# Differential attention of a two-layer hybrid block: new weight sum, new unit order, seven key tiles on GpSimd

## Chip, cores and metric

The kernel runs on one core of one Trainium2 chip. The metric is the device time of the program in microseconds. PE is the TensorE matmul queue and PEld its weight load, DVE is VectorE, ACT is ScalarE, POOL is GpSimd, and SP is the queue that issues most DMAs.

## The reference

Two layers of a block with three attention branches (gated linear, differential, sliding window), an output projection and a SwiGLU. Only the differential branch is touched:

```
s = einsum('bhctd,bhcmd->bhctm', q, k) * DIFF_DH ** -0.5      # 4 heads, c = 2 maps of width 32
p = softmax(s, axis=-1)
w = p[:, :, 0] - lam * p[:, :, 1]
o = einsum('bhtm,bhmv->bhtv', w, v)                            # v is 64 wide
out = rms_norm(o, g) * (1 - lam_init)                          # per head, eps 1e-6
```

There are 256 context and 1024 latent tokens, so 10 tiles of 128. In layer 0 context rows attend to context keys, latent rows to all 1280 keys; in layer 1 only latent rows are needed. Everything is float32.

## The kernel before

The program runs stage after stage with a barrier between them; `differential_attention` runs once per layer, after the gated linear attention and ahead of the sliding window. Each engine has its own instruction stream and works it in program order; engines meet only at semaphores (`wait_ge`, `then_inc`).

The unit of work is one head of one query tile (`u`). A pair of tiles (`i`) has 8 units. Layer 0 has 8 short context units (256 keys) and 32 latent units (1280 keys); layer 1 has 32 latent units. `staggered` writes the steps `r` of a software pipeline: in step `r` an engine does the first part of unit `r` and later parts of earlier units, and `live(lag)` says whether unit `r - lag` exists. The context units and the latent units are two pipelines, each filled and drained by itself.

One unit, before:

- PE L1723: scores of map 0, then of map 1, into the two PSUM halves `SC[:, c]` (3 matmuls each). A half is free again once its exponential is done.
- DVE L1852, L1854: row maximum and its negative. ACT L1777: exponential with the row sum into `den`.
- DVE L1859, L1861: reciprocals of both sums, and minus lambda times the second. POOL L1828: `W = E0 / den0`. DVE L1867: `W += E1 * r1`, over all keys.
- PE L1710: transposes of W in three groups of 3, 4 and 3 tiles. Groups 0 and 2 use PSUM bank `TR[:, 0]`, group 1 uses `TR[:, 1]`. ACT L1785 copies each group to `WT` (`take`).
- PE L1747: ten products of a value tile (128x64) with WT, accumulated in `TR[:, 1]`. DVE L1872 copies the 64x128 result into `oT`.

In step `r` PE issues score 0 and score 1 of `r`, groups 0, 1 and 2 of `r-2`, and the products of `r-3`. ACT does `take` 0 and 1 of `r-2`, exponential 0 of `r`, `take` 2 of `r-2`, exponential 1 of `r`. The stage starts once all constants, the values and the keys have landed; the values are transposed first (L1702, L1765). After the last unit the RMS norm is made on full 128x1280 tiles: squares (L1802), a product with the block mean (L1758), square root (L1805), reciprocal (L1878), product (L1880), for two head pairs.

Of the kernel before, what the change touches and what calls it, by code (L numbers as in the profile page):

```python
# [1595 lines left out]
def differential_attention(nc, t, res, layer, tiles):  # L1596

    with nc.cleanup_on_exit(), ExitStack() as ctx:
# [5 lines left out]
        LAG = 3  # L1610
# [3 lines left out]
        first_latent = CTX_TILES // 2  # L1614
        KEYCH = [(0, 512), (512, 512), (1024, 256)]
# [13 lines left out]
        eps = sb(nm + "eps", [P, 1])  # L1629
        mx = sb(nm + "mx", [P, 2])  # L1630
        ng = sb(nm + "negmax", [P, 2])
        den = sb(nm + "den", [P, 2, 2])
        rden = sb(nm + "rden", [P, 2, 2])
        r1 = sb(nm + "r1", [P, 2])
        E = sb(nm + "e", [P, 2, 2, T])
        W = sb(nm + "w", [P, 2, T])
# [4 lines left out]
        const_in, k_in, eps_set = sem("const_in"), sem("k_in"), sem("eps_set")  # L1641
        q_in = [sem(f"q_in{s}") for s in range(2)]
        lam, lam_exp = sem("lam"), sem("lam_exp")
        v_turned, v_copied = sem("v_turned"), sem("v_copied")
        scores, max_done, neg_done, exp_done, rden_done, r1_done, w0_done, w_done = (
            sem("scores"), sem("max_done"), sem("neg_done"), sem("exp_done"), sem("rden_done"), sem("r1_done"), sem("w0_done"), sem("w_done"))
        turned = [sem(f"turned{g}") for g in range(3)]
        copied = [sem(f"copied{g}") for g in range(3)]
        pv_done, o_done, passed = sem("pv_done"), sem("o_done"), sem("passed")
        sq_done, mean_done, rms_done, inv_done, normed, stored = (  # L1650
            sem("sq_done"), sem("mean_done"), sem("rms_done"), sem("inv_done"), sem("normed"), sem("stored"))
# [4 lines left out]
        def done(i, u):  # L1656

            return (i - first_pair) * UN + u + 1
# [4 lines left out]
        def groups(i):  # L1663

            return [(0, 1), (1, 1)] if is_ctx(i) else [(0, 3), (3, 4), (7, 3)]

        def third(i, u):

            return done(i, u) - (first_latent - first_pair) * UN

        def stagger(eng, step):
            if first_pair < first_latent:
                staggered(eng, first_pair, first_latent, UN, LAG, step)
            staggered(eng, first_latent, end_pair, UN, LAG, step)

        @block.sync
        def _(sp):
            heads = t["heads"]
            for j, part in enumerate((0, 1, 0)):
                sp.dma_start(ks[32 * j:32 * j + 32, :, :].bitcast(F32), heads[part, HEAD_DK:HEAD_DK + 2 * P, 0:T].rearrange("(a p) n -> p a n", p=32)).then_inc(k_in, 16)  # L1680

            def body(i, first):
                for s in range(2):
                    if not first:
                        sp.wait_ge(scores, 2 * (done(i, s * H + H - 1) - UN))
                    for j, part in enumerate((0, 0, 1)):
                        sp.dma_start(qs[32 * j:32 * j + 32, s, :, :].bitcast(F32),
                                     heads[part, HEAD_DQ:HEAD_DQ + 2 * P, bass.ds(i * 2 * P + s * P, P)].rearrange("(a p) n -> p a n", p=32)).then_inc(q_in[s], 16)
# [7 lines left out]
        def _(pe):  # L1696
            pe.wait_ge(const_in, 80)
            for g, (i, a, n) in enumerate(VG):
                if g >= 2:
                    pe.wait_ge(v_copied, g - 1)  # L1700
                for c in range(n):
                    mm = pe.transpose(TR[:, g % 2, c * P:(c + 1) * P], vT[:, i, (a + c) * P:(a + c + 1) * P], ident[:, :])  # L1702
                mm.then_inc(v_turned, 1)
            pe.wait_ge(v_copied, len(VG))
            pe.wait_ge(k_in, 48)

            def turn(i, u, g):
                a, n = groups(i)[g]
                for c in range(n):
                    mm = pe.transpose(TR[:, g % 2, c * P:(c + 1) * P], W[:, u % 2, (a + c) * P:(a + c + 1) * P], ident[:, :])  # L1710
                mm.then_inc(turned[g], 1)

            def step(i, r, live):
                if live(0):
                    s, h = r // H, r % H
                    if h == 0:
                        pe.wait_ge(q_in[s], (i - first_pair) * 48 + 48)
                    for c in range(2):

                        wait_count(pe, exp_done, 2 * (done(i, r) - 1) + c - 1)  # L1720
                        for a, n in KEYCH[:1 if is_ctx(i) else 3]:
                            n = min(n, N_CTX) if is_ctx(i) else n
                            mm = pe.matmul(SC[:, c, a:a + n], qs[:, s, 2 * h + c, :], ks[:, 2 * h + c, a:a + n], start=True, stop=True)  # L1723
                        mm.then_inc(scores, 1)
                if live(2):
                    u = r - 2
# [8 lines left out]
                    if not is_ctx(i):  # L1735
                        pe.wait_ge(copied[0], done(i, u))
                        turn(i, u, 2)
                if live(3):
                    u, h = r - 3, (r - 3) % H

                    pe.wait_ge(copied[1], done(i, u) + (1 if live(2) else 0))
                    wait_count(pe, o_done, done(i, u) - 1)
                    if not is_ctx(i):
                        pe.wait_ge(copied[2], third(i, u))
                    tiles_ = groups(i)[-1][0] + groups(i)[-1][1]
                    for c in range(tiles_):
                        mm = pe.matmul(TR[64 * (h % 2):64 * (h % 2) + 64, 1, 0:P], V[:, c, 64 * h:64 * h + 64],  # L1747
                                       WT[:, u % 2, c * P:(c + 1) * P], start=(c == 0), stop=(c == tiles_ - 1))
                    mm.then_inc(pv_done, 1)
            stagger(pe, step)  # L1750


            for i in range(2):
                pe.wait_ge(sq_done, i + 1)
                for a, n in KEYCH:
                    n = min(n, tn - a)
                    if n > 0:
                        mm = pe.matmul(SC[:, i, a:a + n], block_mean[:, :], E[:, 0, i, a:a + n], start=True, stop=True)  # L1758
                mm.then_inc(mean_done, 1)

        @block.scalar
        def _(act):
            for g, (i, a, n) in enumerate(VG):
                act.wait_ge(v_turned, g + 1)
                act.copy(V[:, a:a + n, i * P:(i + 1) * P], TR[:, g % 2, 0:n * P].rearrange("p (c f) -> p c f", f=P)).then_inc(v_copied, 1)  # L1765
            act.wait_ge(lam, 4)
            act.activation(lexp[:, :], lsum[:, :], ACT.Exp).then_inc(lam_exp, 1)
            act.wait_ge(eps_set, 1)

            def step(i, r, live):  # L1770
                keys = (CTX_TILES if is_ctx(i) else TILES) * P

                def exponentials(c):
                    act.wait_ge(neg_done, 2 * (done(i, r) - 1) + c + 1)
                    if c == 0:
                        wait_count(act, w_done, done(i, r) - 2)
                    act.activation(E[:, r % 2, c, 0:keys], SC[:, c, 0:keys], ACT.Exp, bias=ng[:, c:c + 1], scale=scale,  # L1777
                                   accum_out=den[:, r % 2, c:c + 1]).then_inc(exp_done, 1)
# [8 lines left out]
                if live(2):  # L1787
# [401 lines left out]
```

## Time and profile before

| | us |
|---|---|
| median of 3 runs (4523.80 to 4535.81) | 4533.56 |
| the profiled execution, its own time | 4548.76 |
| its span, first to last instruction | 4547.0 |
| PE busy in the span | 3797.9 |
| DVE busy | 1820.1 |
| ACT busy | 1305.8 |
| POOL busy | 1246.8 |

The profile is one execution. Busy times are sums over all stages; what a stage is worth is read from its own stretch. The two differential stages lie at about 783 to 1054 us and 3149 to 3387 us. The granted TensorE clock is 1.00 for 2.4 GHz and 0.50 for 1.2 GHz.

### The profile page before, as it was taken

The numbers are of one execution on the slowest core, as the hardware profiler recorded it, in microseconds if no ns is written. First come the engines' busy times: TensorE is split into PE (matmuls) and PEld (weight loads), VectorE is DVE, ScalarE is ACT, GpSimd is POOL, SyncE is SP. The second block draws the span as 40 slices with busy tenths as digits, with TensorE's granted clock in tenths as the row PEclk, the third lists the DMA queues.
The fourth block names the chain that finished last, engine by engine and source line by source line (L and its number), as shares of the span: only waits on it lengthen the run. The fifth ranks groups of instructions, "written<-read, shape, count | busy, mean of one in ns | idle before, by whom it ended". The sixth has DMA issues, their size and how long they took to land. (4 is left out here: it accounts for less than half of the span.)

```text
span 4547.0 us, 54135 instructions
## 1 busy us (share of the span) xinstructions
PE 3797.9 (84%) x20674; PEld 3078.6 (68%) x20674; DVE 1820.1 (40%) x2680; ACT 1305.8 (29%) x2275; POOL 1246.8 (27%) x877
## 2 busy tenths in 40 slices
PE   7899597795776999999976798696968669999992
PEld 1588487573655888888861687585747548888881
DVE  1104453696754121121228005543968552122215
ACT  2211332574633101111004211332747441111111
POOL 1211321121334323223223211321213243333332
PEclk9999676797988999999998899676989889999996
DMA  7423211203142111111115223202022321111112
GB/s 255 159 83 114 82 24 35 50 11 87 37 137 86 40 33 42 42 37 37 37 58 206 93 80 122 71 13 67 18 58 45 114 83 47 51 46 50 47 37 88
DMA packets 150767, 320.53 MB, mean 70 GB/s; under 512 B 11745, under 2 KB 72033, under 8 KB 150625
## 3 DMA queue, kind: packets, MB, share of 16 engines
q1 hardware_dynamic: 127944, 260.47, 18.4%
q10 hardware_dynamic: 18456, 44.07, 2.6%
q0 software_dynamic: 4224, 14.09, 1.1%
q8 instruction: 90, 1.47, 0.1%
q14 instruction: 53, 0.43, 0.0%
HBM read 250.20 MB, written 68.39 MB: 70 GB/s over the span
## 5 line engine op out<-in xcount | busy, mean ns | idle before, releaser
L1980 POOL TENSOR_TENSOR ffn_wlo<-ffn_raw,ffn_whi 128x1024 fp32r<-128x1024 f32 x132 | 314.6, 2390 | 800.6 <-ACT ffn_whi L1951 800.6
L2044 DVE TENSOR_TENSOR ffn_hid<-ffn_up,ffn_silu 128x512 f32<-128x512 f32 (+1 forms) x110 | 70.2, 638 | 1049.4 <-PE ffn_up L127 1023.2
L1951 ACT CAST ffn_whi<-ffn_raw 128x1024 fp32r<-128x1024 f32 x132 | 136.4, 1049 | 944.7 <-PE ffn_acc L127 467.4
L2049 DVE TENSOR_TENSOR y<-ffn_acc,y 128x512 f32<-128x512 f32 x396 | 274.0, 692 | 266.6 <-PE ffn_acc L127 266.6
L125 PE MATMUL ffn_gate<-second_uhi,ffn_whi 128*128 128x512 f32 (+1 forms) x880 | 326.2, 371 | 37.3 <-POOL ffn_wlo L1980 37.3
L126 PE MATMUL ffn_gate<-second_ulo,ffn_whi 128*128 128x512 f32 (+1 forms) x880 | 325.9, 370 | 0.0
L127 PE MATMUL ffn_gate<-second_uhi,ffn_wlo 128*128 128x512 f32 (+1 forms) x880 | 325.6, 370 | 0.0
L126 PE MATMUL ffn_up<-second_ulo,ffn_whi 128*128 128x512 f32 (+1 forms) x880 | 324.2, 368 | 0.0
L125 PE MATMUL ffn_up<-second_uhi,ffn_whi 128*128 128x512 f32 (+1 forms) x880 | 324.1, 368 | 0.0
L127 PE MATMUL ffn_up<-second_uhi,ffn_wlo 128*128 128x512 f32 (+1 forms) x880 | 324.0, 368 | 0.0
L125 PE MATMUL ffn_acc<-ffn_whi,ffn_hhi 128*128 128x512 f32 x792 | 308.5, 390 | 0.0
L126 PE MATMUL ffn_acc<-ffn_wlo,ffn_hhi 128*128 128x512 f32 x792 | 308.5, 389 | 0.0
L127 PE MATMUL ffn_acc<-ffn_whi,ffn_hlo 128*128 128x512 f32 x792 | 308.4, 389 | 0.0
L611 POOL TENSOR_TENSOR in_wlo<-in_raw,in_whi 128x1024 fp32r<-128x1024 f32 x42 | 100.3, 2390 | 475.5 <-ACT in_whi L635 475.5
L125 PEld LDWEIGHTS ffn_gate<-second_uhi,ffn_whi 128*128 128x128 f32 x880 | 167.1, 190 | 66.4 <-POOL ffn_wlo L1980 38.1
L1011 PE MATMUL gla_unit<-gla_X 64*128 64x64 f32 x1120 | 209.1, 365 | 0.0
L1010 PE MATMUL gla_unit<-gla_X 64*128 64x64 f32 x1120 | 209.1, 365 | 0.0
L1010 PEld LDWEIGHTS gla_unit<-gla_X 64*128 64x128 f32 x1120 | 200.7, 277 | 7.7 <-DVE gla_A L1265 2.7
L1852 DVE TENSOR_REDUCE diff_mx<-diff_scores 128x1 f32<-128x1280 f32 (+1 forms) x144 | 196.8, 1367 | 11.5 <-PE diff_scores L1723 10.3
L1011 PEld LDWEIGHTS gla_unit<-gla_X 64*128 64x128 f32 x1120 | 200.7, 277 | 0.0
L685 DVE LOAD_MASK_SELECT in_swap<-in_stage x18 | 0.3, 14 | 497.9 <-ACT in_stage L640 497.9
L125 PE MATMUL in_acc<-second_uhi,in_whi 128*128 128x512 f32 (+1 forms) x504 | 179.9, 357 | 20.9 <-POOL in_wlo L611 20.9
(269 smaller groups left out, 9172.0 us busy)
## 6 DMA issues: line engine op xcount, KB each, us to landing
ffn_raw<-w_ffn_dram SPq DMA_DIRECT2D x132, 512.0 KB, 3.5
in_raw<-w_in_dram SPq DMA_DIRECT2D x42, 512.0 KB, 3.5
norm_input_ada_w<-w_ada_dram SPq DMA_DIRECT2D x10, 2048.0 KB, 8.1
norm_ffn_ada_w<-w_ada_dram SPq DMA_DIRECT2D x8, 2048.0 KB, 8.8
proj_scratch<-in_stage ACTq DMA_DIRECT2D x24, 640.0 KB, 2.9
ada_w<-w_ada_dram SPq DMA_DIRECT2D x6, 2048.0 KB
heads_scratch<-in_shi ACTq DMA_DIRECT2D x18, 640.0 KB, 3.0
heads_scratch<-in_slo ACTq DMA_DIRECT2D x18, 640.0 KB, 4.2
```

The lines of the kernel that those rows point to most:

```text
L125: pe.matmul(out, st_hi, mv_hi, start=start, stop=False)
L126: pe.matmul(out, st_hi, mv_lo, start=False, stop=False)
L127: return pe.matmul(out, st_lo, mv_hi, start=False, stop=stop)
L611: pool.tensor_tensor(wlo[:, s, :, :], raw[:, s, :].rearrange("p (k n) -> p k n", k=KT), whi[:, s, :, :].bitcast(F32), ALU.subtract).then_i ...
L685: dve.stream_shuffle(swap[:, s, :], x, MASK).then_inc(swapped, 1)
L1010: pe.matmul(fslot(s, c), x[UP, :], halves(x, m)[UP, :, 1, :], start=True, stop=True)
L1011: mm = pe.matmul(bslot(s, c), x[DOWN, :], halves(x, m)[DOWN, :, 0, :], start=True, stop=True)
L1852: dve.reduce_max(mx[:, c:c + 1], SC[:, c, 0:keys], AX.X).then_inc(max_done, 1)
L1951: act.copy(whi[:, j % 3, :], raw[:, j % 3, :]).then_inc(w_hi, 1)
L1980: pool.tensor_tensor(wlo[:, j % 3, :], raw[:, j % 3, :], whi[:, j % 3, :].bitcast(F32), ALU.subtract).then_inc(w_ready, 1)
L2044: dve.tensor_tensor(hf[:, c, 0:tn], UP[:, c, 0:tn], sg[:, c, 0:tn], ALU.mult).then_inc(mul_done, 1)
L2049: dve.tensor_tensor(Y[:, tt, cols], ACC[:, half, :], Y[:, tt, cols], ALU.add).then_inc(y_added, 1)
```

## The change

It rewrites the body of `differential_attention`. The weights are no longer divided by the first sum: `W = E0 + ratio * E1` with `ratio = -lam * den0 / den1`, and the first sum enters only the norm, where its square multiplies epsilon. The parts:

- Weights: POOL multiplies and then adds over the first 7 key tiles (896 columns, two instructions); DVE does the last 3 tiles (384 columns) in one instruction. W has 4 buffers in place of 2.
- Order: on PE score 0 of `r`, group 2 of `r-3`, products of `r-4`, score 1 of `r`, groups 0 and 1 of `r-2`. On ACT exponential 0 of `r`, `take` 0 and 1 of `r-3`, exponential 1 of `r`, `take` 2 of `r-3`. The drain is 4 steps in place of 3.
- Products: the ten key tiles go in two chains of five, one to PSUM partitions 0 to 63 and one to 64 to 127, issued in turn; DVE copies one half and adds the other.
- Start: queries of the first tile are loaded first, keys by head with a semaphore each, values by a DMA of the ACT queue; the values are transposed and lambda is made after the first unit's scores.
- Norm: means and square roots on 128x20 numbers, spread to full tiles by small products.

The core of the diff (removed lines are shown where the order on ACT changes; elsewhere the listing above has them):

```
-        LAG = 3
+        TURN, REST, WEIGH = 2, 3, 4
...
+        OWN = 7
...
+        W = sb(nm + "w", [P, 4, T])
...
+                    if first and s == 0:
+                        for h in range(H):
+                            keys(h)
...
+            def values():
+                pe.wait_ge(v_in, 16)
+                for g, (i, a, n) in enumerate(VG):
+                    if g >= 2:
+                        pe.wait_ge(v_copied, g - 1)
+                    for c in range(n):
+                        mm = pe.transpose(TR[:, g % 2, c * P:(c + 1) * P], vT[:, i, (a + c) * P:(a + c + 1) * P], ident[:, :])
+                    mm.then_inc(v_turned, 1)
...
                 if live(0):
+                    if r % H == 0:
+                        pe.wait_ge(q_in[r // H], (i - first_pair) * 48 + 48)
+                    if isinstance(i, int):
+                        pe.wait_ge(k_in[r % H], 48)
+                    score(i, r, 0)
+                if live(REST) and not is_ctx(i):
+                    u = r - REST
+                    pe.wait_ge(copied[0], done(i, u))
+                    pe.wait_ge(w2_done, third(i, u))
+                    turn(i, u, 2)
+                if live(WEIGH):
+                    u, h = r - WEIGH, (r - WEIGH) % H
+                    pe.wait_ge(copied[1], done(i, u) + (1 if live(REST) else 0))
+                    pe.wait_ge(copied[0], done(i, u))
+                    wait_count(pe, o_done, done(i, u) - 1)
+                    if not is_ctx(i):
+                        pe.wait_ge(copied[2], third(i, u))
+                    n = (groups(i)[-1][0] + groups(i)[-1][1]) // 2
+                    for c in range(n):
+                        for half in range(2):
+                            k = half * n + c
+                            mm = pe.matmul(TR[64 * half:64 * half + 64, 1, 0:P], V[:, k, 64 * h:64 * h + 64],
+                                           WT[:, u % 2, k * P:(k + 1) * P], start=(c == 0), stop=(c == n - 1))
+                    mm.then_inc(pv_done, 1)
+                if live(0):
+                    score(i, r, 1)
+                    if first_step(i, r):
+                        values()
+                if live(TURN):
+                    u = r - TURN
                     pe.wait_ge(w_done, done(i, u))
                     wait_count(pe, copied[0], done(i, u) - 1)
                     if not is_ctx(i):
                         wait_count(pe, copied[2], third(i, u) - 1)
                     turn(i, u, 0)
+                    wait_count(pe, copied[1], done(i, u) - 1)
                     wait_count(pe, o_done, done(i, u) - (1 if live.starts and u == 0 else 2))
                     turn(i, u, 1)
             stagger(pe, step)
...
+                for c in tiles:
+                    mm = pe.matmul(TR[:, i, 2 * c:2 * c + 2], E[:, 0, i, c * P:(c + 1) * P], block_mean[:, 0:P:64], start=True, stop=True)
                 mm.then_inc(mean_done, 1)
+            for i in range(2):
+                pe.wait_ge(inv_done, i + 1)
+                for c in tiles:
+                    for half in range(2):
+                        mm = pe.matmul(SC[64 * half:64 * half + 64, i, c * P:(c + 1) * P], rs[:, i, c, half:half + 1].to_broadcast([P, 64]), ident[:, :], start=True, stop=True)
+                mm.then_inc(spread_done, 1)
...
+            act.dma_start(vT[:, :, :], t["proj"][T_DV * P:(T_DV + 2) * P, 0:T].rearrange("(i p) n -> p i n", p=P)).then_inc(v_in, 16)
...
-                if live(2):
-                    take(r - 2, 0)
-                    take(r - 2, 1)
                 if live(0):
                     exponentials(0)
-                if live(2) and not is_ctx(i):
-                    take(r - 2, 2)
+                if live(REST):
+                    take(r - REST, 0)
+                    take(r - REST, 1)
                 if live(0):
                     exponentials(1)
+                if live(REST) and not is_ctx(i):
+                    take(r - REST, 2)
+                if first_step(i, r):
+                    act.wait_ge(lam, 4)
+                    act.activation(lexp[:, :], lsum[:, :], ACT.Exp).then_inc(lam_exp, 1)
+                    for g, (j, a, n) in enumerate(VG):
+                        act.wait_ge(v_turned, g + 1)
+                        act.copy(V[:, a:a + n, j * P:(j + 1) * P], TR[:, g % 2, 0:n * P].rearrange("p (c f) -> p c f", f=P)).then_inc(v_copied, 1)
             stagger(act, step)
...
+                    n = min(keys, OWN * P)
+                    w = W[:, u % 4, 0:n]
+                    pool.tensor_scalar(w, E[:, u % 2, 1, 0:n], ratio[:, u % 2:u % 2 + 1], 1.0, ALU.mult, ALU.mult).then_inc(w1_done, 1)
+                    pool.wait_ge(w1_done, done(i, u))
+                    pool.tensor_tensor(w, w, E[:, u % 2, 0, 0:n], ALU.add).then_inc(w_done, 1)
             stagger(pool, step)
...
+                if live(0):
+                    maximum(i, r, 0)
                 if live(1):
                     u, b = r - 1, (r - 1) % 2
+                    at = (tile_of(i, u), slice(u % H, u % H + 1))
+                    dve.wait_ge(exp_done, 2 * done(i, u))
+                    dve.reciprocal(rden[:, b:b + 1], den[:, 1, at[0], at[1]].rearrange("p a b -> p (a b)")).then_inc(rden_done, 1)
+                    dve.wait_ge(rden_done, done(i, u))
+                    wait_count(dve, w_done, done(i, u) - 2)
+                    dve.scalar_tensor_tensor(ratio[:, b:b + 1], den[:, 0, at[0], at[1]].rearrange("p a b -> p (a b)"), nlam[:, 0:1], rden[:, b:b + 1], ALU.mult, ALU.mult).then_inc(ratio_done, 1)
+                    if not is_ctx(i):
+                        wait_count(dve, turned[2], third(i, u) - 4)
+                        dve.wait_ge(ratio_done, done(i, u))
+                        dve.scalar_tensor_tensor(W[:, u % 4, OWN * P:T], E[:, u % 2, 1, OWN * P:T], ratio[:, b:b + 1],
+                                                 E[:, u % 2, 0, OWN * P:T], ALU.mult, ALU.add).then_inc(w2_done, 1)
+                if live(0):
+                    maximum(i, r, 1)
+                    if first_step(i, r):
+                        difference()
+                if live(WEIGH):
+                    u = r - WEIGH
+                    h = u % H
+                    rows, other = slice(64 * (h % 2), 64 * (h % 2) + 64), slice(64 - 64 * (h % 2), 128 - 64 * (h % 2))
+                    at = bass.ds(i * 2 * P + u // H * P, P)
                     dve.wait_ge(pv_done, done(i, u))
+                    dve.tensor_copy(oT[rows, h // 2, at], TR[rows, 1, 0:P]).then_inc(half_done, 1)
+                    dve.wait_ge(half_done, done(i, u))
+                    dve.tensor_tensor(oT[rows, h // 2, at], oT[rows, h // 2, at], TR[other, 1, 0:P], ALU.add).then_inc(o_done, 1)
             stagger(dve, step)
...
+            seen = slice(tiles[0], TILES)
+            dve.tensor_tensor(dsq[:, seen, :], den[:, 0, seen, :], den[:, 0, seen, :], ALU.mult).then_inc(dsq_done, 1)
+            dve.wait_ge(dsq_done, 1)
+            for i in range(2):
+                dve.wait_ge(mean_done, i + 1)
+                dve.scalar_tensor_tensor(ms[:, i, seen, :], dsq[:, seen, 2 * i:2 * i + 2], EPS,
+                                         TR[:, i, 2 * tiles[0]:2 * TILES].rearrange("p (c a) -> p c a", a=2), ALU.mult, ALU.add).then_inc(ms_done, 1)
+            for i in range(2):
+                dve.wait_ge(rms_done, i + 1)
+                dve.reciprocal(rs[:, i, seen, :], ms[:, i, seen, :]).then_inc(inv_done, 1)
             for i in range(2):
                 o = oT[:, i, t0:t0 + tn]
```

## Rows read from the trace of the kernel before

**Rows 1.** The page: the granted TensorE clock over the span's 40 slices.

```profile
PEclk9999676797988999999998899676989889999996
```

**Rows 2.** Busy time by stretch: start us:end us, length, PE, PEld, DVE, ACT, POOL, clock, DMA.

```profile
842.00:862.00 20.00, 14.92 (x48) 11.09 (x49) 16.02 (x23) 12.61 (x21) 4.00 (x3) 0.50 0.07 20
862.00:1014.00 152.00, 147.12 (x1022) 120.32 (x1021) 145.66 (x226) 114.41 (x198) 37.28 (x28) 1.00 0.05 14
1090.00:1240.00 150.00, 124.91 (x770) 102.08 (x769) 125.81 (x292) 113.78 (x259) 53.70 (x72) 1.00 0.18 41
```

**Rows 3.** Groups of DVE instructions, 862 to 1014 us: busy, mean ns, idle before.

```profile
L1852 DVE TENSOR_REDUCE diff_mx<-diff_scores 128x1 f32<-128x1280 f32 x56 | 83.1, 1485 | 1.0 <-PE diff_scores L1723 0.5
L1867 DVE SCALAR_TENSOR_TENSOR diff_w<-diff_e,diff_r,diff_w 128x1280 f32<-128x1280 f32 x28 | 43.5, 1552 | 0.4 <-issue 0.3
L1854 DVE TENSOR_SCALAR diff_negmax<-diff_mx 128x1 f32<-128x1 f32 x56 | 8.6, 154 | 1.9
L1872 DVE COPY diff_oT<-diff_tr 64x128 f32 (+1 forms) x29 | 8.3, 285 | 2.7 <-PE diff_tr L1747 2.3
L1861 DVE TENSOR_SCALAR diff_r<-diff_rden,diff_nlam 128x1 f32<-128x1 f32 x28 | 6.0, 214 | 1.0
```

**Rows 4.** Instructions in order of time, one full-clock unit: start us, us, engine.

```profile
907.35 0.80 PEld L1710 LDWEIGHTS diff_tr<-ident,diff_w 128*128 128x128 f32 x7
...
908.00 1.02 ACT L1785 COPY diff_wT<-diff_tr 128x384 f32<-128x384 f32 x2 [1.26 <-PE diff_tr L1710]
...
909.07 2.40 PE L1747 MATMUL diff_tr<-diff_wT,diff_V 128*64 128x128 f32 x20
```

**Rows 5.** The same view, latent units of layer 0 at the half clock.

```profile
840.00 1.49 DVE L1852 TENSOR_REDUCE diff_mx<-diff_scores 128x1 f32<-128x1280 f32 x1 [1.07 <-PE diff_scores L1723]
...
843.18 1.44 PE L1723 MATMUL diff_scores<-diff_k,diff_q 96*128 96x512 f32 x3 [2.15 <-ACT diff_e L1777]
...
844.65 1.49 DVE L1852 TENSOR_REDUCE diff_mx<-diff_scores 128x1 f32<-128x1280 f32 x1 [1.39 <-PE diff_scores L1723]
...
846.37 1.33 ACT L1777 ACTIVATE diff_e<-diff_scores,diff_negmax 128x1280 f32<-128x1280 f32 x1 [1.65 <-DVE diff_negmax L1854]
...
853.19 1.33 ACT L1777 ACTIVATE diff_e<-diff_scores,diff_negmax 128x1280 f32<-128x1280 f32 x1
...
854.51 0.48 ACT L1785 COPY diff_wT<-diff_tr 128x384 f32<-128x384 f32 x1
...
859.96 2.39 PE L1747 MATMUL diff_tr<-diff_wT,diff_V 128*64 128x128 f32 x10
```

**Rows 6.** The same view, small products of the linear attention in two column halves.

```profile
705.14 4.12 PE L1057 MATMUL gla_unit<-ident,gla_rs 128*64 128x128 f32 x40
```

**Rows 7.** Groups of POOL instructions over the whole span.

```profile
L535 POOL TENSOR_TENSOR norm_attention_h<-norm_attention_h,norm_attention_lng 128x1024 f32<-128x1024 f32 x18 | 43.0, 2387 | 114.5 <-ACT norm_attention_h L491 114.5
L1828 POOL TENSOR_SCALAR diff_w<-diff_e,diff_rden 128x1280 f32<-128x1280 f32 x64 | 85.2, 1332 | 298.0 <-DVE diff_rden L1859 290.2 <-PE diff_tr L1710 4.2 <-issue 3.6
```

**Rows 8.** The last latent unit's first maximum and the end of the loop, layer 0.

```profile
1008.65 1.49 DVE L1852 TENSOR_REDUCE diff_mx<-diff_scores 128x1 f32<-128x1280 f32 x1
...
1024.77 0.29 DVE L1872 COPY diff_oT<-diff_tr 64x128 f32<-64x128 f32 x1 [2.51 <-PE diff_tr L1747]
```

**Rows 9.** Start of the stage: layer 0, DMA of 785 to 812 us; then layer 1.

```profile
805.61 0.30 DVE L1836 TENSOR_TENSOR diff_lprod<-diff_lamv 128x32 f32<-128x32 f32 x2 [26.13 <-DMA diff_block_mean<-block_mean_dram]
DMA packets 2831, 6.07 MB, mean 225 GB/s; under 512 B 256, under 2 KB 1792, under 8 KB 2831
3149.65 0.44 SPq L1680 DMA_DIRECT2D diff_k<-heads_scratch  x1
3176.41 2.50 PE L1723 MATMUL diff_scores<-diff_k,diff_q 96*128 96x512 f32 x6 [0.46 <-ACT diff_V L1765]
```

**Rows 10.** The norm at the end of the stage, layer 0, in order of time.

```profile
1030.23 8.15 DVE L1878 RECIPROCAL diff_e<-diff_e 128x1280 f32<-128x1280 f32 x1 [5.17 <-ACT diff_e L1805]
```

**Rows 11.** One line: small DVE instructions with two SBUF inputs; ns min/median/max.

```profile
L426 DVE SCALAR_TENSOR_TENSOR norm_attention_nmu<-norm_attention_mv,norm_attention_rstd x36: 159/160/2380, 1292.6 to 3713.1; 128x1 f32<-128x1 f32 x36
```

More of the change, by code:

```diff
@@ L1678, in _, with queries, keys @@
             heads = t["heads"]
-            for j, part in enumerate((0, 1, 0)):
-                sp.dma_start(ks[32 * j:32 * j + 32, :, :].bitcast(F32), heads[part, HEAD_DK:HEAD_DK + 2 * P, 0:T].rearrange("(a p) n -> p a n", p=32)).then_inc(k_in, 16)
+            def queries(i, s):
+                for j, part in enumerate((0, 0, 1)):
+                    sp.dma_start(qs[32 * j:32 * j + 32, s, :, :].bitcast(F32),
+                                 heads[part, HEAD_DQ:HEAD_DQ + 2 * P, bass.ds(i * 2 * P + s * P, P)].rearrange("(a p) n -> p a n", p=32)).then_inc(q_in[s], 16)
+            def keys(h):
+                rows = slice(HEAD_DK + 64 * h, HEAD_DK + 64 * h + 64)
+                for j, part in enumerate((0, 1, 0)):
+                    sp.dma_start(ks[32 * j:32 * j + 32, 2 * h:2 * h + 2, :].bitcast(F32), heads[part, rows, 0:T].rearrange("(a p) n -> p a n", p=32)).then_inc(k_in[h], 16)
             def body(i, first):
@@ L1713, in step, with score @@
+            def score(i, r, c):
+                h = r % H
+                wait_count(pe, exp_done, 2 * (done(i, r) - 1) + c - 1)
+                for a, n in KEYCH[:1 if is_ctx(i) else 3]:
+                    n = min(n, N_CTX) if is_ctx(i) else n
+                    mm = pe.matmul(SC[:, c, a:a + n], qs[:, r // H, 2 * h + c, :], ks[:, 2 * h + c, a:a + n], start=True, stop=True)
+                mm.then_inc(scores, 1)
             def step(i, r, live):
                 if live(0):
-                    s, h = r // H, r % H
@@ L1716, in step @@
[L1716 to L1724, printed above, removed]
@@ L1731, in step @@
                     turn(i, u, 0)
+                    wait_count(pe, copied[1], done(i, u) - 1)
                     wait_count(pe, o_done, done(i, u) - (1 if live.starts and u == 0 else 2))
                     turn(i, u, 1)
[L1735 to L1749, printed above, removed]
@@ new lines, in maximum @@
+            def maximum(i, r, c):
+                keys = (CTX_TILES if is_ctx(i) else TILES) * P
+                n = 2 * (done(i, r) - 1) + c + 1
+                dve.wait_ge(scores, n)
+                dve.reduce_max(mx[:, c:c + 1], SC[:, c, 0:keys], AX.X).then_inc(max_done, 1)
+                dve.wait_ge(max_done, n)
+                dve.tensor_scalar(ng[:, c:c + 1], mx[:, c:c + 1], -scale, None, ALU.mult).then_inc(neg_done, 1)
+            def step(i, r, live):
+                if live(0):
+                    maximum(i, r, 0)
@@ new lines, in step @@
+                    if not is_ctx(i):
+                        wait_count(dve, turned[2], third(i, u) - 4)
[6 more added lines that the diff above has]
+                        difference()
```

135 lines of the change are left out of this document (48 added, 87 removed).

## Prediction, made blind

> **What bounds the kernel now.** I read the clock line of the page first [rows 1]: it moves between its two levels, so each stretch needs its own. Then busy time by stretch. From 862 to 1014 us the latent loop of layer 0 has the full clock with DVE busy for 145.66 of 152 us and PE for 147.12 [rows 2]. Two engines are nearly full. The groups of DVE say how full: per unit two maxima (2 x 1.485), two negatives (2 x 0.154), two reciprocals, the lambda product (0.214), the weight sum (1.552) and the copy to `oT` (0.285) [rows 3]. The 28 units in 152 us make 5.43 us each. First maximum of the first to first maximum of the last latent unit, 840.00 [rows 5] to 1008.65 [rows 8], is 168.65 us for 31 steps, 5.44 each. DVE waits for nobody longer than half a microsecond there, because each unit's chain of waits is spread over three steps: ACT does `take` 0 and 1 of an old unit before exponential 0 of the new one, so no engine waits for work of its own step.
>
> **The new order closes a ring.** I wrote down for each engine what its new stream needs, in step `r`:
>
> 1. PE: score 0 of `r`. Then group 2 of `r-3` waits for `copied[0]`, which is `take` 0 of `r-3`.
> 2. ACT issues that `take` behind exponential 0 of `r`, so it waits for maximum 0 of `r`, so for score 0 of `r`.
> 3. PE: the products of `r-4` wait for `copied[1]` of `r-3`; score 1 of `r` stands behind them.
> 4. ACT issues `take` 2 of `r-3` behind exponential 1 of `r`: that needs maximum 1, so score 1.
> 5. PE: group 0 of `r-2` waits for `copied[2]` of `r-3`, and score 0 of `r+1` stands behind groups 0 and 1.
>
> So score 0, maximum 0, exponential 0, two copies, products, score 1, maximum 1, exponential 1, one copy, seven transposes, score 0 of the next unit: all in series, with no slack from any lag. More buffers for W don't open it, since no wait in it is for W.
>
> **Its length at the half clock.**
> - Maximum start to exponential start: 844.65 to 846.37, 1.72 us [rows 5], twice.
> - Exponential to the end that releases the copy behind it: 853.19 to 854.51, 1.32 [rows 5], twice.
> - Two copies, to the first product: 908.00 to 909.07, 1.07 [rows 4]; group 2's three transposes run beside the second copy and push the products by about 0.18.
> - Products: the nearest row is 20 pairs of column halves in 4.12 us [rows 6], 0.206 a pair, if the halves of a pair overlap as there. Five pairs plus drain of the pipeline would be 1.3, ten passes without overlap 2.39 [rows 5]. The listing issues ten products of 128 columns; I take 2.3, nearer to the unpaired end.
> - One copy of 384 columns: 0.48, with handover 0.53 [rows 5].
> - Seven transposes at the 0.21 to 0.24 a pass that ten passes show [rows 5]: 1.5, plus 0.1 to start.
> - Score start to maximum start: 843.18 to 844.65, 1.47 [rows 5], twice.
>
> First half 1.72 + 1.32 + 1.25 + 2.3 + 1.47 = 8.06; second 1.72 + 1.32 + 0.53 + 1.6 + 1.47 = 6.64. Together **14.7 us a unit**. The path through `o_done` is shorter: it asks for maximum 1 and some 2 us of DVE, where exponential 1 and `take` 2 need 3.6 from the same start.
>
> **Its length at the full clock.** ACT and DVE keep their durations. Products 1.25 (twenty passes in 2.40 [rows 4]), score to maximum about 0.85 (half of the three passes' 1.44 [rows 5], and 0.13 to hand over), seven transposes 0.80 [rows 4]: **11.5 us**.
>
> **Which clock.** PE would be busy about 7.4 of 14.7 us at the half clock, and 4.2 of 11.5 at the full one. The stretch 842 to 862 had PE busy for 14.92 of 20 and stayed at 0.50; 124.91 of 150 kept 1.00 in another stage [rows 2]. Both are far above 50%, so I take the half clock.
>
> The Trainium skill ("TensorE: Matmul & The Clock Gate", section "A second HAM failure mode: psum-queue depth-cycling") says that PE's short idles between groups of matmuls make the clock go up and down instead of settling. By that rule part of the loop would have the full clock; the stretch at 0.50 here shows no such change.
>
> **The sum, against the profiled execution (4548.76 us).**
> - Latent loop, per layer: the first three steps have no work of older units, 16 us at about the 5.4 of now; the fourth is a ring without products, 12.4; 27 steps of 14.7 make 397. Then 30 us from the last unit's first maximum to the last `oT` (13.2 left of its step, four drain steps of some 4.2), where before it took 16.41 (1008.65 to 1025.06 [rows 8]). 455 against 185: +270, for two layers **+540**.
> - Context units, layer 0: the ring has no `take` 2, so only its first half closes. With a fifth of the maximum, exponential and products that leaves 3.7 us, plus 1.4 for score 1, two transposes and the next score: 5.1, against some 2.6. Eight of them +20. The start gives back part: DVE waited 26.13 us for the last constant [rows 9]; the loads are 6.07 MB at 225 GB/s [rows 9], so the first head and tile are there after about half of that, but the last keys set the fourth unit. I take -17; bounds 0 and -26. Together **+3**.
> - Start of layer 1: first scores 26.8 us after the issue of the keys (3149.65 to 3176.41 [rows 9]); now first keys and queries alone after about 13. Less 3 for the values in the first step: **-11** (bounds 0 and -14).
> - Norm: each layer loses an 8.15 us reciprocal [rows 10] and, by the durations of exponentials and scores, about 5 of full-width square root and wide mean products; it gains 20 passes for the means and 20 pairs for the spreading, about 4.3 each at 0.21 [rows 6]. The last products stay. **-8** for both (bounds -14 and 0).
> - POOL at 7 tiles: the multiply is 1332 ns for 1280 columns, the addition 2387 for 1024 [rows 7], so for 896 columns 1.01 and 2.11 (the second by the wider type of operation, nearest row). DVE's 384 columns 0.62. These 3.1 us run beside the ring: W is needed two steps later. Nothing; were the ring open, POOL would still need less than DVE.
> - DVE's new copy and addition of halves: 0.57 in place of 0.285, beside the ring: nothing.
>
> 540 + 3 - 11 - 8 = +524. The profiled execution is 15 us, 0.3%, above the median, so the sum is set on the median: 4533.56 + 524 = **5058 us**.
>
> **Rivals.**
> - *The ring at the full clock, or part of it.* Speaks for it: the loop enters from stages with their own clock, and idle time within a unit is spread in short pieces. Against: the busy share above. At 11.5 us a unit the latent loops cost +354 and starts and norm -22: 4866; with half of the loop at each clock some 4960. Chance 0.22 for anything from 4866 to 5000.
> - *Faster: no ring, DVE bounds.* This needs `take` of `r-3` to be done before exponential 0 of `r`, which decides at that one wait: if PE's group 2 of `r-3` need not stand ahead of score 1 in time, or my reading of the counts is off by a unit. Then DVE needs 2 x 1.485 + 2 x 0.154 + 0.155 + 0.21 + 0.62 + 0.57 [rows 3], 4.8 us, and PE with pairs about 4. 63 steps of -0.55 are -34, starts and norm -24: 4475. Chance 0.09.
> - *Same: that, but DVE's part of W waits for POOL.* DVE's instructions with two SBUF inputs last 160 ns as a rule and up to 2380 [rows 11], as long as the addition of POOL in the same stretch. If DVE's 384 columns waited for a multiply of 1.01 each unit it would need 5.85, and 63 x 0.4 would eat the gains: 4543 or so. Both wait for the same ratio, and DVE follows its own release sooner. Chance 0.02. The Trainium skill ("SBUF — State Buffer") has the port pair of DVE and GpSimd as an exclusive lock, held for the full instruction; in the ring this costs nothing, since DVE has over 8 us of slack a unit.
> - *Longer.* Products at 2.39 and more, each handover 0.1 longer: 16 us a unit, 5140. Chance 0.04.
>
> **How the numbers follow.** The ring at the half clock has 0.63. Its own range is 5000 to 5110: 14.7 give or take 0.9 a unit over 58 steps is 52 us. The range reaches down to 4870, which takes in the ring at the full clock, and ends at 5110. Left out are the faster case, the same, and the longer one. A measurement of this kernel can tell about 0.3% from no change. Faster 0.09, same 0.02, slower 0.89.
>
> **What would show it.** In the changed profile first maxima should stand 14.7 us apart in the latent loops (11.5 if the clock is full). PE should wait for ACT's copies to `diff_wT` ahead of the products and of group 0, and for nothing of W; ACT should wait for DVE's negatives and start its copies at once behind each exponential; DVE busy under 40% of the loop; the clock 0.50 there; POOL two instructions near 1.0 and 2.1; no reciprocal of 8 us; first scores some 13 us after the issue of loads. I am wrong if the copies lie ahead of their step's exponentials in time, or if first maxima come under 6 us apart.

## The result and the profile after

| | before, us | after, us |
|---|---|---|
| median (4 runs each) | 4534.69 | 5055.74 |
| lowest to highest | 4523.80 to 4542.01 | 5040.69 to 5060.31 |
| profiled execution: span | 4547.0 | 5052.8 |

The ratio is 1.1145 (95% interval 1.1113 to 1.1178): 11% slower. The prediction of 5058 us is 2 us off. The page of the changed kernel, busy times and clock:

```profile
PE 3908.7 (77%) x20870; PEld 3148.9 (62%) x20870; DVE 1768.8 (35%) x2750; ACT 1301.6 (26%) x2275; POOL 1385.2 (27%) x945
...
PEclk9998675555798899999998997865556988999996
```

DVE has less work than before (1820.1) and ACT as much. PE is busy for 111 us more and POOL for 138 us more, while the span is 506 us longer: most of the added time is work that waits, not more work. The low digits in the clock line, against [rows 1], are the two stages. The loop of layer 0 by stretch (columns as in [rows 2]):

```profile
880.00:1260.00 380.00, 186.95 (x935) 141.84 (x936) 123.72 (x230) 104.41 (x182) 90.07 (x52) 0.57 0.02 5
```

PE is busy for 49% and DVE for 33%, where [rows 2] had 97% and 96%. The groups of PE, ACT and DVE in the latent units of layer 0, with what ended their idle time:

```profile
L1710 PE MATMUL diff_tr<-ident,diff_w 128*128 128x128 f32 x320 | 81.5, 419 | 218.7 <-ACT diff_wT L1809 214.2 <-DVE diff_w L1896 3.8 <-DVE diff_oT L1910 0.7
...
L1801 ACT ACTIVATE diff_e<-diff_scores,diff_negmax 128x1280 f32<-128x1280 f32 x64 | 84.9, 1327 | 313.6 <-DVE diff_negmax L1880 313.6
...
L1878 DVE TENSOR_REDUCE diff_mx<-diff_scores 128x1 f32<-128x1280 f32 x63 | 93.9, 1491 | 272.7 <-PE diff_scores L1728 272.7
```

Each engine has one partner: PE waits for ACT's copies, ACT for DVE's negatives, DVE for PE's scores. That is a ring, and the order in time shows one turn of it:

```profile
1104.91 1.49 DVE L1878 TENSOR_REDUCE diff_mx<-diff_scores 128x1 f32<-128x1280 f32 x1 [4.25 <-PE diff_scores L1728]
...
1106.81 1.33 ACT L1801 ACTIVATE diff_e<-diff_scores,diff_negmax 128x1280 f32<-128x1280 f32 x1 [4.87 <-DVE diff_negmax L1880]
...
1107.19 0.62 DVE L1896 SCALAR_TENSOR_TENSOR diff_w<-diff_e,diff_ratio 128x384 f32<-128x384 f32 x1
1107.29 1.39 POOL L1854 TENSOR_SCALAR diff_w<-diff_e,diff_ratio 128x896 f32<-128x896 f32 x1 [11.44 <-DVE diff_ratio L1892]
...
1108.12 0.95 ACT L1809 COPY diff_wT<-diff_tr 128x384 f32<-128x384 f32 x2
...
1109.55 2.40 PE L1755 MATMUL diff_tr<-diff_wT,diff_V 128*64 128x128 f32 x20
...
1111.88 0.86 PE L1728 MATMUL diff_scores<-diff_k,diff_q 96*128 96x512 f32 x3
1112.77 1.49 DVE L1878 TENSOR_REDUCE diff_mx<-diff_scores 128x1 f32<-128x1280 f32 x1 [4.97 <-PE diff_scores L1728]
...
1114.58 1.33 ACT L1801 ACTIVATE diff_e<-diff_scores,diff_negmax 128x1280 f32<-128x1280 f32 x1 [5.50 <-DVE diff_negmax L1880]
...
1115.89 0.47 ACT L1809 COPY diff_wT<-diff_tr 128x384 f32<-128x384 f32 x1
...
1116.51 1.73 PE L1710 MATMUL diff_tr<-ident,diff_w 128*128 128x128 f32 x7 [3.77 <-ACT diff_wT L1809]
...
1117.89 1.42 PE L1728 MATMUL diff_scores<-diff_k,diff_q 96*128 96x512 f32 x3
1119.34 1.49 DVE L1878 TENSOR_REDUCE diff_mx<-diff_scores 128x1 f32<-128x1280 f32 x1 [4.32 <-PE diff_scores L1728]
```

Within the ring nothing overlaps; only work outside it runs beside it (W, group 2's transposes, the output). From 1104.91 to 1119.34 are 14.43 us; over the last 27 steps the first maxima stand 14.73 us apart in layer 0 and 14.64 in layer 1. DVE's wait of 4.97 ends with three score passes of 0.86 in all, so at the full clock. The clock was granted at 1.00 for short stretches, of which most fell on an idle PE: cut into pieces of half a microsecond, 880 to 1260 us has the full clock in 100 of 760, and in those PE was busy for 11% of the time, against 55% in the pieces at the half clock. By the rows of the two kernels, each stage splits like this (us; before, after, and what was forecast for the difference):

| | before | after | difference | forecast |
|---|---|---|---|---|
| layer 0: first load issued to first latent maximum | 56.5 | 58.9 | +2.4 | +3 |
| layer 1: the same | 29.5 | 16.4 | -13.1 | -11 |
| first to last latent unit's first maximum, layers 0, 1 | 168.6, 168.3 | 424.3, 427.5 | | |
| from there to the last output copy | 16.4, 16.4 | 25.9, 26.1 | | |
| both together, both layers | 369.8 | 903.8 | +534 | +540 |
| norm, to the second store, both layers | 44.8 | 32.4 | -12.4 | -8 |

Their sum is +511; the rest of the span gives 5 back.

### The profile page after: what moved, and what is told of

Its sections match the earlier page's. It is cut to its first block and busy times, and to the rows that moved or that the text cites. A ratio compares the mean times of both kernels' runs of the same rounds, so it can differ in the third digit from the quotient of the medians.

```text
span 5052.8 us, 55157 instructions
## 1 busy us (share of the span) xinstructions
PE 3908.7 (77%) x20870; PEld 3148.9 (62%) x20870; DVE 1768.8 (35%) x2750; ACT 1301.6 (26%) x2275; POOL 1385.2 (27%) x945
## 5 line engine op out<-in xcount | busy, mean ns | idle before, releaser
L1710 PE MATMUL diff_tr<-ident,diff_w 128*128 128x128 f32 x656 | 170.2, 420 | 441.5 <-ACT diff_wT L1809 431.3
L1710 PEld LDWEIGHTS diff_tr<-ident,diff_w 128*128 128x128 f32 x656 | 119.0, 214 | 499.9 <-issue 254.0
L1801 ACT ACTIVATE diff_e<-diff_scores,diff_negmax 128x1280 f32<-128x1280 f32 (+1 forms) x144 | 177.4, 1232 | 670.2 <-DVE diff_negmax L1880 670.2
L1854 POOL TENSOR_SCALAR diff_w<-diff_e,diff_ratio 128x896 f32<-128x896 f32 (+1 forms) x72 | 91.7, 1274 | 716.1 <-DVE diff_ratio L1892 611.8
L1728 PE MATMUL diff_scores<-diff_k,diff_q 96*128 96x512 f32 (+1 forms) x400 | 179.1, 576 | 54.5 <-DMA diff_k<-heads_scratch 45.0
L1011 PE MATMUL gla_unit<-gla_X 64*128 64x64 f32 x1120 | 201.2, 355 | 0.0
```

The lines of the kernel that those rows point to most:

```text
L1011: mm = pe.matmul(bslot(s, c), x[DOWN, :], halves(x, m)[DOWN, :, 0, :], start=True, stop=True)
L1728: mm = pe.matmul(SC[:, c, a:a + n], qs[:, r // H, 2 * h + c, :], ks[:, 2 * h + c, a:a + n], start=True, stop=True)
```

## The experiments

In all of them the period is the mean distance of first maxima over the last 27 latent steps of a layer. Times are medians against runs of the kernel before on the same chip, whose medians lay between 4530 and 4538 us.

**1. Copies first.**

```
+                if live(REST):
+                    take(r - REST, 0)
+                    take(r - REST, 1)
                 if live(0):
                     exponentials(0)
-                if live(REST):
-                    take(r - REST, 0)
-                    take(r - REST, 1)
+                if live(REST) and not is_ctx(i):
+                    take(r - REST, 2)
                 if live(0):
                     exponentials(1)
-                if live(REST) and not is_ctx(i):
-                    take(r - REST, 2)
```

> The changed kernel with ACT's three copies of r-3 ahead of the exponentials of r, as the kernel before has them; all else stays. Theory (two closed rings through ACT): both open, first maxima 4.8 to 5.0 us apart, DVE near full, full clock in the loops, total about 4480 (4460 to 4510). Rival A (the order on PE alone closes it): still over 8 us a unit, total above 4700. Rival B (GpSimd's multiply and addition hold W back once the ring is open): 5.4 to 5.9 us a unit, total 4525 to 4560.

The edit puts two copies ahead of both exponentials and the third between them, which is where the kernel before has it.

Measured: 4636.99 us, ratio to the kernel before 1.0238 (1.0201 to 1.0274), period 7.77 and 7.57 in layers 0 and 1. ACT's order alone takes back 419 of 521 us, so rival A falls. But neither the period nor the total came near the theory's 4.8 to 5.0 and 4480 us. The rows of one step:

```profile
953.64 0.29 DVE L1908 COPY diff_oT<-diff_tr 64x128 f32 x1
...
953.97 0.28 DVE L1910 TENSOR_TENSOR diff_oT<-diff_oT,diff_tr 64x128 f32 x1
...
954.40 0.63 PE L1710 MATMUL diff_tr<-ident,diff_w 128*128 128x128 f32 x4 [2.18 <-DVE diff_oT L1910]
954.76 0.79 PEld L1728 LDWEIGHTS diff_scores<-diff_k,diff_q 96*128 96x128 f32 x3
```

PE's group 1 waits 2.18 us for the output addition, which stands behind maximum 1 on DVE, so behind score 1, so behind the products; score 0 of the next unit stands behind group 1. This is the path through `o_done` that the prediction called shorter: it was, and it is next. Single periods in layer 0 lie between 6.6 and 8.5 us from the sixth step on, at a mean clock of 0.77.

**2 and 3. Half of the ring each.** Experiment 2 puts copies 0 and 1 first but leaves copy 2 behind both exponentials; experiment 3 leaves ACT as changed and issues `score(i, r, 1)` right behind `score(i, r, 0)`.

> Copies 0 and 1 of r-3 first, then both exponentials, copy 2 still last. Theory: the first half of the ring opens, the second stays: scores 0 (1.42), group 2 (0.65), products (2.4), score 1 to maximum 1.45, to exponential 1.85, 1.31, copy 0.62, seven transposes 1.4: 11.1 us a unit at the half clock, total about 4860 (4740 if the full clock comes in at 8.9). Rival (one wait alone decides): under 6 us, total below 4550, or unchanged at 14.7.

> The changed kernel with score 1 right behind score 0 on PE, ACT's order as changed. Theory: the two halves of the ring run side by side up to the exponentials, what is left is 1.45 + 4.7 (maximum 0 to exponential 1 with DVE's weights between) + 1.31 + 0.62 + 1.4, about 9.6 us a unit, total 4770 to 4790 (4700 if the clock is full). Rival (order on ACT alone matters, score 1 has slack): no change, 5040 to 5070.

Measured: 4793.54 us (1.0573), period 10.18 and 10.19; and 4743.15 us (1.0462), period 9.52 and 9.40. No single wait decides: opening either half alone takes back 262 or 313 us. In experiment 2 the clock was 0.67 on average in the loop, and the result lies between the two values written down for the half and the full clock. Experiment 3, with a clock of 0.71, came within 0.2 us of its period but 27 us below its total; the run does not show which term was too long.

**4. The kernel before with copies late**, the one edit of experiment 1 turned round:

> The kernel before with one thing of the change: on ACT, copies 0 and 1 behind exponential 0 and copy 2 behind exponential 1. Theory: the order on ACT closes a ring there too: score 0 to maximum, exponential, copies, products of r-3, score 0 of r+1, 7.8 us at the full clock and 10.8 at the half, total 4680 to 4870. Rival (the ring needs the new order on PE as well, ACT's order has slack): 5.4 to 5.6 us a unit, total within 10 of 4535.

Measured: 4674.87 us, 1.0311 (1.0262 to 1.0361), period 7.68 in both layers, by the 7.8 of the full clock (0.94 granted). So the place of ACT's copies costs 137 us even without the rest of the change, about a quarter of the loss. The ring that it closes there is shorter, because PE's order is still the old one.

**5. Outputs first.** Experiment 1, and on DVE the copy and addition of `r-4` ahead of `maximum(i, r, 1)`.

> The kernel of the first experiment (copies first) with DVE's copy and addition of the output of r-4 moved ahead of maximum 1 of r. In that experiment PE's group 1 still waited for the output addition, which stood behind maximum 1, which needs score 1, which stands behind the products: a third ring, 7.44 us. Theory: it opens too, what is left is DVE's own 4.8 us a unit at the full clock, 4.8 to 5.1, total 4480 to 4500 (62 steps of 2.5 less than 4637). Rival (GpSimd's 3.5 us and the way through W set the pace): 5.5 to 6, total 4530 to 4550. Rival (clock stays low): over 6.5, total above 4580.

Measured: 4595.58 us, 1.0143 (1.0114 to 1.0172), period 6.80. A miss: 4.8 to 5.1 was expected. The third ring opened and a fourth took over. Its rows at the full clock:

```profile
949.57 1.33 ACT L1801 ACTIVATE diff_e<-diff_scores,diff_negmax 128x1280 f32<-128x1280 f32 x1 [2.36 <-DVE diff_negmax L1880]
...
950.89 0.96 ACT L1809 COPY diff_wT<-diff_tr 128x384 f32<-128x384 f32 x2
...
951.96 1.31 PE L1755 MATMUL diff_tr<-diff_wT,diff_V 128*64 128x128 f32 x20
...
953.20 0.85 PE L1728 MATMUL diff_scores<-diff_k,diff_q 96*128 96x512 f32 x3
...
954.09 1.49 DVE L1878 TENSOR_REDUCE diff_mx<-diff_scores 128x1 f32<-128x1280 f32 x1
...
955.90 1.33 ACT L1801 ACTIVATE diff_e<-diff_scores,diff_negmax 128x1280 f32<-128x1280 f32 x1 [2.36 <-DVE diff_negmax L1880]
```

Exponential 1, copies 0 and 1, products, score 1, maximum 1, exponential 1: 6.33 us, because score 1 stands behind the products and these behind copies that follow the last exponential.

**6. PE filled with needless work.**

```
                     score(i, r, 0)
+                    if live(REST) and not is_ctx(i):
+                        wait_count(pe, exp_done, 2 * (done(i, r) - 1) + 0)
+                        for _k in range(28):
+                            pe.transpose(SC[:, 1, 0:P], ident[:, :], ident[:, :])
```

and the same behind score 1, into the other half.

> The changed kernel with 28 needless transposes of the identity behind score 0 and 28 behind score 1 in the latent loops, into the half of the scores that is free, where PE stood idle 3.8 us each time. Their values are overwritten or never read; nothing is left out. Theory (same ring, only PE's parts run at the clock): PE busy over 80%, full clock, 11.5 to 11.9 us a unit, total 4870 to 4910. Rival (the ring's length is in the waits and PE's parts do not matter, or the added work lengthens it): 14.7 or more, total 5055 or above.

Measured: 4878.52 us (1.0765), period 11.67 and 11.60. The stretch has PE busy for 211 of 240 us and the full clock:

```profile
860.00:1100.00 240.00, 211.25 (x1892) 191.52 (x1891) 98.47 (x182) 82.97 (x143) 70.55 (x41) 1.00 0.04 11
```

So 177 of the 521 us lost go with the clock, and the ring at the full clock has the length that the prediction gave it (11.5).

**7. One chain of products.**

> The changed kernel with the ten products in one chain to one half of the PSUM partitions, and DVE's copy alone (no addition), as the kernel before has them. Ten products are twenty passes in the profile. If the two halves of a pair overlap, the products take 2.4 us as changed and 4.7 in one chain at the half clock: 17.0 us a unit, total 5055 + 59 x 2.3, about 5190. If they do not overlap: unchanged, 5040 to 5070. If the fuller PE raises the clock, in between: 5100 to 5150.

Measured: 5117.57 us (1.1292), period 16.14 and 15.89. That is the third case written down, in between. Two units, one with the full clock in part of it:

```profile
1153.20 3.43 PE L1753 MATMUL diff_tr<-diff_wT,diff_V 128*64 128x128 f32 x20
...
1167.58 4.53 PE L1753 MATMUL diff_tr<-diff_wT,diff_V 128*64 128x128 f32 x20
```

4.53 against 2.40 us for the same twenty passes at the half clock: the halves of a pair overlap. The fuller PE got a mean clock of 0.63 in place of 0.57, which gives part of it back.

**8 and 11. Other shares for GpSimd:** `OWN = 9` and `OWN = 4`.

> The changed kernel with 9 key tiles on GpSimd and 1 on DVE in place of 7 and 3. Theory (W has a whole step of slack in the ring): GpSimd 4.4 us a unit in place of 3.5, and the time does not move, 5040 to 5070. Rival (group 0 waits for GpSimd in some steps): +0.9 us a unit, total 5100 to 5115.

> The changed kernel with 4 key tiles on GpSimd and 6 on DVE. In the changed kernel GpSimd's multiply takes 1.38 us for 896 columns, with 9 tiles 1.33 for 1152, though 256 take 0.48 and 1280 in the kernel before 1.33. Theory: GpSimd waits inside that instruction for DVE's part of W, which starts 0.1 us before it and also reads two tiles: with 768 columns (about 1.02 us) on DVE the multiply of 512 columns takes 1.4 to 1.6 us. Rival (a fixed price of this multiply): 0.70 us by its width. The time of the kernel does not move under either, 5040 to 5070.

Measured: 5049.34 us (1.1142), period 14.76 and 14.65, with 9 tiles; 5033.14 us (1.1106), period 14.73 and 14.66, with 4. The second total lies 7 us below its range, but its ratio to the kernel before has an interval (1.1040 to 1.1173) that overlaps that of the changed kernel (1.1113 to 1.1178), and the period has not moved. W is beside the ring, whichever engine makes it. GpSimd's multiply, with 7, 9 and 4 tiles:

```profile
L1854 POOL TENSOR_SCALAR diff_w<-diff_e,diff_ratio 128x896 f32<-128x896 f32 x32 | 44.0, 1376 | 333.9 <-DVE diff_ratio L1892 275.6 <-issue 58.3
```

```profile
L1854 POOL TENSOR_SCALAR diff_w<-diff_e,diff_ratio 128x1152 f32<-128x1152 f32 x32 | 42.6, 1332 | 318.7 <-DVE diff_ratio L1892 263.2 <-issue 55.5
```

```profile
L1854 POOL TENSOR_SCALAR diff_w<-diff_e,diff_ratio 128x512 f32<-128x512 f32 x29 | 42.0, 1447 | 337.8 <-DVE diff_ratio L1892 293.4 <-issue 44.4
```

The fewer its columns, the longer it takes, as DVE's part grows: with 9, 7 and 4 tiles on GpSimd, DVE's part takes 0.35, 0.62 and 1.02 us.

**10. The old order with all else of the change.** PE, ACT and the lags as in the kernel before.

> All parts of the change but its order, with the order of the kernel before: PE scores 0 and 1 of r, groups 0, 1, 2 of r-2, products of r-3; ACT copies 0 and 1 of r-2, exponential 0, copy 2, exponential 1. Theory: the kernel before has a ring of its own beside the full DVE (exponential 1 of r-1, score 1 of r 0.95, groups 0 and 1 about 0.8, copies to exponential 0 1.07, exponential 0 1.31, copy 2 0.5, exponential 1 1.31: 5.4 to 5.9 us), so DVE's relief gives nothing a unit: 5.3 to 5.5 us, total 4495 to 4510 by the start and the norm alone. Rival (before is bound by DVE's work alone): 4.8 to 5.0 us a unit, total 4470 to 4485.

Measured: 4484.52 us, 0.9904 (0.9867 to 0.9940), period 5.34 and 5.32, where the kernel before has 5.35 and 5.34 by the same count, although W takes 0.93 us less of DVE in each unit. So the period came as the theory had it, and the rival (4.8 to 5.0) falls by it; the total did not: 4484.52 lies 10 us below the theory's range and at the edge of the rival's. DVE is no longer full, and neither is PE:

```profile
880.00:980.00 100.00, 80.31 (x684) 59.63 (x682) 88.89 (x171) 75.83 (x132) 65.43 (x38) 1.00 0.06 16
```

One turn of what sets the pace instead:

```profile
920.88 1.33 ACT L1799 ACTIVATE diff_e<-diff_scores,diff_negmax 128x1280 f32<-128x1280 f32 x1
...
922.36 0.85 PE L1728 MATMUL diff_scores<-diff_k,diff_q 96*128 96x512 f32 x3 [0.93 <-ACT diff_e L1799]
...
923.04 0.93 PE L1710 MATMUL diff_tr<-ident,diff_w 128*128 128x128 f32 x7
...
923.57 1.02 ACT L1807 COPY diff_wT<-diff_tr 128x384 f32<-128x384 f32 x2 [1.27 <-PE diff_tr L1710]
...
924.49 1.33 ACT L1799 ACTIVATE diff_e<-diff_scores,diff_negmax 128x1280 f32<-128x1280 f32 x1
...
925.80 0.48 ACT L1807 COPY diff_wT<-diff_tr 128x384 f32<-128x384 f32 x1
...
926.16 1.35 ACT L1799 ACTIVATE diff_e<-diff_scores,diff_negmax 128x1280 f32<-128x1280 f32 x1
```

Exponential 1, score 1 of the next unit into the half that it frees, groups 0 and 1, their copies, exponential 0, copy 2, exponential 1: 5.28 us. The kernel before has the same links (its copies also wait 1.26 us for PE's transposes [rows 4]), so there this ring and a full DVE were about equally long. Of the 46 us won, the two stages show 34 in the profiles (first load to second store, 468 against 501): start and norm. The other 12 are not explained; what lies outside the two stages took between 4008 and 4046 us in seven of the profiles.

**9 and 12. A spread order.** PE: score 0 of `r`, groups 0, 1, 2 of `r-3`, score 1 of `r`, products of `r-4`; ACT as in experiment 1, DVE as changed. Experiment 12 adds `OWN = 9`.

```
                     score(i, r, 0)
+                if live(REST):
+                    u = r - REST
...
+                    turn(i, u, 0)
...
+                    turn(i, u, 1)
...
+                        turn(i, u, 2)
+                if live(0):
+                    score(i, r, 1)
```

> All parts of the change but its order. PE: score 0 of r, groups 0, 1 and 2 of r-3, score 1 of r, products of r-4. ACT: copies 0 and 1 of r-3, exponential 0 of r, copy 2 of r-3, exponential 1 of r. DVE as changed. In the experiment with outputs first a fourth ring was left (exponential 1 of r-1, copies 0 and 1 of r-3, group 2, products of r-4, score 1 of r, maximum 1, exponential 1 of r: 6.27 us at the full clock). Theory: here score 1 stands ahead of the products and the turned groups are two steps old, so no ring is longer than DVE's own 4.8 us: 4.8 to 5.1 us a unit, full clock, total 4475 to 4500, faster than the kernel before. Rival (the clock falls once PE has more idle time than before): over 5.5 us in part of the loop, total 4520 to 4560.

> The spread order with 9 key tiles on GpSimd and 1 on DVE. Theory: there maximum 1 starts 0.65 us after score 1 is done because DVE still makes its part of W, so DVE's 0.27 us less comes off each unit: 4.8 to 5.0 us, total 10 to 16 less than the spread order. Rival (group 1 behind the output addition and ACT's copies set 5.1 us, or GpSimd's later W does): no change or up to 0.3 us a unit more.

Measured: 4501.50 us, 0.9925 (0.9898 to 0.9951), period 5.24 and 5.25; and 4481.76 us, 0.9895 (0.9847 to 0.9944), period 5.03 and 4.95. Both are faster than the kernel before, by about 1%. The first is slower than its theory in period and total, by 0.1 us and 2 us; the second has a median 20 us below the first's, on another chip, where 10 to 16 were expected, and its period in layer 0 is just above its range. The step of 0.2 to 0.3 us a unit between them fits the 0.27 us that DVE's part of W became shorter. In experiment 9 maximum 1 started at 958.01, when DVE had finished that part, while score 1 had ended at 957.36; in a stretch of 130 us, 44 maxima waited for PE's scores for 0.2 us in all. In the profiles the two stages together take 454 us with 7 tiles and 441 with 9, against 462 for the old order and 483 for the kernel before (first load to first store); the ratios of 9, 10 and 12 have overlapping intervals. By the stages experiment 9 is shorter than 10, by the medians 17 us longer, so which of the two orders is the better program is not settled.

## Why the prediction was right, and where it was not

- **The ring** is shown: its waits in the groups, its turn in the timeline, both halves by experiments 1 to 3, and the weight of ACT's order by experiment 4. 14.7 us a unit was forecast, 14.73 and 14.64 came.
- **Its terms** are less exact than the sum. Maximum to exponential took 1.90 and 1.81, not 1.72; copies to products 1.43, not 1.25. Seven transposes with their start took 1.4 to the next score, not 1.6, since the score starts before the last has ended, and the full clock now and then shortened a score by 0.6. The errors cancel; that the sum lies within 0.1 us is in part luck. So is the total's distance of 2 us: the stages came 13 us below the forecast (loops 6, start and norm 7), and the two profiled executions differ by 506 us, not by the 524 of the sum. The medians differ by 521, because the profiled execution of the kernel before was a long one.
- **The products** were mis-reasoned. The prediction took five pairs or ten passes for a unit; a unit has twenty passes, ten pairs. The ten passes of [rows 5] were half a unit, as the twenty of [rows 4] show. By the same rows the bounds should have been 2.1 (ten pairs) and 4.8 (twenty passes); the value taken, 2.3, came close to the 2.40 measured because halves overlap, not because it lay near the unpaired end (experiment 7, 4.53). That it held was luck.
- **The clock** was half as forecast, but not throughout: 0.57 on average. The rival of a changing clock did occur in small; in experiment 5 too single periods of layer 0 jump, between 5.8 and 8.9 us, at a mean clock of 0.89. The Trainium skill ("TensorE: Matmul & The Clock Gate", section "A second HAM failure mode: psum-queue depth-cycling") tells of a kernel whose clock goes up and down because PE idles briefly between groups of matmuls. The traces agree. The number that matters here is another: the mean clock was only 0.07 above the half clock, and the full clock throughout would be worth 177 us (experiment 6).
- **The faster rival** named one wait to decide. That was wrong: behind ACT's order lay two more rings, one of 7.6 to 7.8 us on average at the clock it ran at (experiment 1) and one of 6.3 us at the full clock (experiment 5). A period of 5.2 us took ACT's old order together with a new order on PE (experiment 9), and 5.3 the old order on both (experiment 10). The sum of the rival "same" does not come out either: 25 us of loop less the 24 of start and norm that the rival "faster" takes gives 4535, not 4543.
- **What bounded the kernel before** was put down to DVE. Experiment 10 shows a ring of the same length: with DVE busy for 89% and PE for 80% the period stayed. The prediction read a full DVE and stopped there.
- **Start, drain, norm**: 13 us forecast to the first scores, 15 and 15 came; the drain took 26 us, not 30; the norm gave 12.4, not 8. All small beside +534.
- **W beside the ring costs nothing**: shown by experiments 8 and 11, though the multiply took 1.38 us in place of the 1.01 forecast (last section).
- **The wait of GpSimd and DVE for each other**, priced against DVE in the rival "same", mostly fell on GpSimd (experiments 8 and 11). The Trainium skill ("SBUF — State Buffer", section "🔬 SBUF: two separate sides") says that GpSimd shares a pair of ports with DVE, and that whichever instruction starts first, GpSimd's or one of DVE's with two inputs in SBUF, holds the pair to its end. The trace agrees in both directions (last section).

## What to carry to other kernels

Write each engine's stream as a list and follow the waits round: if one turn comes back to the same step, its length bounds the period, whatever the busy times say. More buffers do not open it where none of its waits is for a buffer (W had four here). What an older unit needs should be issued ahead of what waits for this step's work, on every engine it passes; and when one ring is opened, price the next before forecasting the gain. An engine that is full may share its bound with a ring of equal length, and then relieving the engine gains nothing.

## What the runs showed of the hardware beyond that

GpSimd's multiply of 512 columns (1.45 us) took longer than of 1152 (1.33). As a rule it starts 0.1 us after DVE's part of W, and its record is long as if it waited inside it for DVE to end; that was forecast before the run with 4 tiles (1.4 to 1.6 against 0.70). Once in the changed kernel GpSimd came first, and the price changed sides:

```profile
959.35 1.01 POOL L1854 TENSOR_SCALAR diff_w<-diff_e,diff_ratio 128x896 f32<-128x896 f32 x1 [11.34 <-DVE diff_ratio L1892]
959.46 1.31 DVE L1896 SCALAR_TENSOR_TENSOR diff_w<-diff_e,diff_ratio 128x384 f32<-128x384 f32 x1 [0.32 <-DVE diff_ratio L1892]
```

The multiply then took 1.01 us, DVE's 384 columns 1.31 in place of 0.62. The later instruction's record is 0.15 to 0.2 us shorter than the rest of the other one and its own time together (1.38 against 0.52 + 1.01, 1.31 against 0.90 + 0.62); what overlaps there is not shown.

PE's records show two products at a time when they write to different halves of the partitions: 20 passes in 2.40 us against 4.53, and 1.31 against 2.40 at the full clock [rows 4].
